# The first expert's low parts on VectorE around the row table, in a two-layer encoder on one Trainium2 core

## The reference

```
lg = x2 @ w_group + b_group            # the group of a token: argmax
le = x2 @ w_router + b_router          # its two experts within the group: top_k
...
order = jnp.argsort(flat_e)            # tokens sorted by expert, in blocks of rows
...
def expert_block(args):
    xb, e = args
    hid = jax.nn.silu(xb @ w_gate[e]) * (xb @ w_up[e])
    return hid @ w_down[e]
...
out = jnp.zeros_like(x2).at[slot_tok].add(ys * slot_w[:, None])
```

## Time and profile before

| | us |
|---|---|
| three runs | 2655.75, 2651.90, 2654.62 |
| median | 2654.62 |
| the profiled execution's own time | 2650.67 |
| its span, first to last instruction | 2649.0 |
| layer 0: first small DVE instruction behind the logits, first gate product | 502.60, 560.24 |
| the same in layer 1 | 1964.03, 2022.70 |
| busy by the page: PE, DVE, ACT, POOL | 2327.3, 1896.5, 1550.3, 331.2 |

### The profile page before, as it was taken

One profiled execution on the slowest core, in us unless ns is written; L12 is line 12 of the kernel. 1 busy time (PEld: TensorE's weight loads), 2 busy tenths in 40 slices (PEclk: granted clock), 3 DMA queues, 4 the chain that ended last, 5 costly groups with the idle time before them and its releaser, 6 DMA issues. The chain is left out here.

```text
span 2649.0 us, 34467 instructions
## 1 busy us (share of the span) xinstructions
PE 2327.3 (88%) x11464; PEld 1759.8 (66%) x11464; DVE 1896.5 (72%) x2453; ACT 1550.3 (59%) x2036; POOL 331.2 (13%) x268
## 2 busy tenths in 40 slices
PE   7899989459999999929999999998955999999991
PEld 5666658447777776727787777776843777777771
DVE  6775572668988888858566676556266988898885
ACT  5554450437787777725555555555042787778772
POOL 0000020211222111030000000002021222122102
PEclk9999999779999999969999999999976999999996
DMA  3013020649999999852000000002154999999995
GB/s 120 25 52 98 24 72 32 212 151 390 393 404 397 395 392 401 348 172 88 24 24 24 24 24 24 0 24 72 32 197 149 378 403 396 397 396 402 396 369 210
DMA packets 129503, 538.49 MB, mean 203 GB/s; under 512 B 23233, under 2 KB 52033, under 8 KB 80289
## 3 DMA queue, kind: packets, MB, share of 16 engines
q1 hardware_dynamic: 110496, 470.62, 46.7%
q0 software_dynamic: 18944, 67.12, 7.3%
HBM read 487.50 MB, written 50.20 MB: 203 GB/s over the span
## 5 line engine op out<-in xcount | busy, mean ns | idle before, releaser
L1508 DVE TENSOR_TENSOR m_lo_gate<-m_raw_gate,m_hi_gate 128x2048 fp32r<-128x2048 f32 x128 | 289.1, 2289 | 99.6 <-ACT m_hi_gate L1503 99.5
L1503 ACT CAST m_hi_down<-m_raw_down 128x2048 fp32r<-128x2048 f32 x124 | 236.2, 1906 | 106.6 <-PEq L848 67.1
L1508 DVE TENSOR_TENSOR m_lo_down<-m_raw_down,m_hi_down 128x2048 fp32r<-128x2048 f32 x124 | 279.5, 2283 | 10.6 <-ACT m_hi_down L1503 10.2
L1508 DVE TENSOR_TENSOR m_lo_up<-m_raw_up,m_hi_up 128x2048 fp32r<-128x2048 f32 x124 | 283.1, 2283 | 4.8 <-ACT m_hi_up L1503 4.3
L1503 ACT CAST m_hi_gate<-m_raw_gate 128x2048 fp32r<-128x2048 f32 x132 | 246.7, 1906 | 17.9 <-DMA m_raw_gate<-in_moe_w_gate_dram 17.9
L1503 ACT CAST m_hi_up<-m_raw_up 128x2048 fp32r<-128x2048 f32 x128 | 244.5, 1912 | 18.0 <-DMA m_raw_up<-in_moe_w_up_dram 17.1
L1622 PE MATMUL m_G<-m_hi_gate,m_x_hi 128*96 128x512 f32 x512 | 206.2, 403 | 11.4 <-DVE m_x_lo L1732 11.3
L1591 POOL DMA_INDIRECT m_xg<-hn_rows,m_pick x64 | 154.7, 2417 | 417.9 <-PE m_XT L1635 403.0
L1622 PE MATMUL m_U<-m_hi_up,m_x_hi 128*96 128x512 f32 x512 | 205.2, 401 | 0.0
L1623 PE MATMUL m_G<-m_hi_gate,m_x_lo 128*96 128x512 f32 x512 | 204.9, 400 | 0.0
L1624 PE MATMUL m_G<-m_lo_gate,m_x_hi 128*96 128x512 f32 x512 | 202.9, 396 | 0.0
(11 more groups left out here) (382 smaller groups left out, 4989.2 us busy)
## 6 DMA issues: line engine op xcount, KB each, us to landing
m_raw_gate<-in_moe_w_gate_dram SPq DMA_DIRECT2D x128, 1024.0 KB, 10.7
m_raw_up<-in_moe_w_up_dram SPq DMA_DIRECT2D x128, 1024.0 KB, 12.6
m_raw_down<-in_moe_w_down_dram SPq DMA_DIRECT2D x124, 1024.0 KB, 10.5
out_rows<-m_y POOLq DMA_DIRECT2D x64, 384.0 KB, 7.9
a1n_rows<-in_diff_w_qkv_dram SPq DMA_DIRECT2D x21, 512.0 KB, 5.3
out_rows<-a0n_gain SPq DMA_DIRECT2D x1, 8064.0 KB, 37.0
x_res<-in_x_dram SPq DMA_DIRECT2D x4, 1024.0 KB, 9.7
a0n_rows<-in_swa_w_o_dram SPq DMA_DIRECT2D x8, 512.0 KB, 3.3
```

Source lines behind the costliest of these rows:

```text
L1503: act.copy(self.hi[w][:, cut], self.raw[w][:, cut]).then_inc(self.hi_done[w], 1)
L1508: eng.tensor_tensor(self.lo[w][:, cut], self.raw[w][:, cut], self.hi[w][:, cut].bitcast(F32), ALU.subtract)\
```

## The change

DVE makes the four low parts of the first expert's gate and up that POOL made. The first (gate 0) stands in route, between the copy of `control` and the copy of the table. The second (gate 1) and third (up 0) stand at the start of run, ahead of `x_part(0)`. The fourth (up 1) stands behind `x_part(0)`, and so do the two of down, which stood ahead of it before. SP's four loads of expert 1's gate and up move from route into run, ahead of the two of down that stood there. POOL has no low part left.

```
@@ route, SP @@
                 for w in range(1, 3):
                     for piece in range(2):
                         moe.load(sp, w, piece, 0)
-                for w in range(2):
-                    for piece in range(2):
-                        sp.wait_ge(moe.lo_done[w], piece + 1)
-                        moe.load(sp, w, piece, 1)
                 norm.sync_stored(sp)
@@ route, POOL @@
-                for w in range(2):
-                    for piece in range(2):
-                        moe.low_part(pool, w, 0, piece)
@@ route, DVE @@
                 own(dve.tensor_copy(moe.control[:, :], ctl_f[0:1, :]))
+                moe.low_part(dve, 0, 0, 0)
                 dve.wait_ge(tabled, 1)
                 own(dve.tensor_copy(moe.table[:, :], L_ps[0:CAP, 0, 0:COLS]))
@@ run, SP @@
                     last = steady_blocks(sp) + 2
-                    for piece in range(2):
-                        load(2, piece, 1, 1)
+                    for w in range(3):
+                        for piece in range(2):
+                            load(w, piece, 1, 1)
@@ run, DVE @@
+                    self.low_part(dve, 0, 0, 1)
+                    self.low_part(dve, 1, 0, 0)
+                    x_part(0)
+                    self.low_part(dve, 1, 0, 1)
                     self.low_part(dve, 2, 0, 0)
                     self.low_part(dve, 2, 0, 1)
-                    x_part(0)
                     last = in_turn(dve, step)
```

## The result

| | before | changed |
|---|---|---|
| median of the runs, us | 2655.35 (6 runs) | 2639.65 (6 runs, 2634.28 to 2641.32) |
| ratio | | 0.9935, 95% interval 0.9924 to 0.9945 |
| the profiled execution's own time, span | 2650.67, 2649.0 | 2641.32, 2639.3 |

The changed kernel is faster by 0.65%, some 17 us (15 to 20 by the interval). The difference of the medians is 15.7.

The account below looks back on a forecast made before the run. In route, DVE's chain of small instructions was taken as the bound, its adds waiting for POOL; the experts' stage had PE busy and DMA saturated. -33.9 + 0.6 + 14.4 = -18.9 us gave 2635.7 against the median, range 2626 to 2643.

Parts of the forecast that it names:

- What is removed: Route: the eight adds of L987 no longer wait for POOL's low parts; 16.7 and 17.2 us, 33.9 in all.
- E: Start of run: the moment at which ACT starts behind the barrier, 550.91 and 2013.72 in the profile before.
- The low part in route: Route: DVE's low part of 2.3 us hides behind the table's matmuls in layer 1, overshoots by 0.6 in layer 0.
- The port at the start of run: Start of run: DVE's two low parts hold POOL's copy and first gather, issued by E + 6.1 instead of E + 3.0.
- The landing in company: Start of run: with three loads ahead, the first gather lands 7.1 us behind its issue instead of 3.17.
- What moves at no cost: Run, behind `x_part`: up 1, the two of down and the loads behind them cost nothing; the cover is 4 us.
- Held up less: Rival, 0.23 with its variants: loads at the start of run do not delay the first gather's landing; -26.7 us, 2627.9.
- The copy alone held: Rival, 0.09: at the start of run low parts delay POOL's copy but not the gather's issue; -22.1 us, 2632.5.
- The adds not held by POOL: Rival, 0.04: in route something else stretches the adds, 33.9 stays and 15.0 us are paid; 2669.6.
- The head start: Rival, 0.04: four loads leaving route's idle stretch are missed in the experts' stage, 21.2 us come back; 2656.9.
- More is paid than I see: Rival, 0.09: a second low part before POOL's copy, a later clock in block 0 or later landing; 5 to 12 us.

Follow-up runs that it names:

- the repetition: The changed kernel, unchanged, run again for a second profile: 0.9929 (0.9916 to 0.9943) against the kernel before, 18.8 us faster.
- the moved loads alone: The kernel before with only SP's four loads of expert 1's gate and up moved from route into run: 1.0041 (1.0026 to 1.0056), 10.9 us slower.
- the kernel before again: The kernel before, unchanged, run once more for a second profile: 2654.07 us.

## Why the prediction was right

Forecast 2635.7 with 2626 to 2643, measured 2639.65 in the six runs and 2634.94 in the five of the repetition. The working said -18.9 us, the ratios say -17.3 and -18.8, and the seams of the two profiles, where all of it was to happen, -18.2 and -18.6.

- **What is removed**, 33.9: 16.7 us in layer 0 as forecast. In layer 1 the way from the first instruction to E is 17.6 shorter, of which 17.3 are the adds. The rest is the clock: the table's matmuls took 4.73 us there and not the 5.44 of the kernel before, so that they ended ahead of the low part.
- **The low part in route**, 0.6 and 0: the way to E in layer 0 is 16.2 us shorter, which is 16.7 less 0.6. Right, with the reservation that the cover is the table's matmuls, and that their length depends on the clock, 4.3 to 5.4 us over the twelve profiles.
- **The port at the start of run**, E + 6.1 between 5.5 and 6.7: E + 5.5 in layer 0, E + 5.4 in layer 1. The first of the two orders happened in both layers: the copy came in between the two low parts. Only one of the two holds it, though they stand back to back. The prediction could not choose between the two orders and took the middle, 0.6 us too late. The Trainium skill (SBUF — State Buffer, Who interferes with whom) infers that such a `tensor_tensor` leaves descriptor generation alone. For the indirect DMA this does not settle the matter: its lengths of 2.20, 2.42, 2.41 and 3.07 us all follow from when a low part ends, and with no low part begun ahead of it it took 1.10. For GpSimd's direct DMA, the store of y, the trace agrees (0.52 to 0.56 us beside a low part, above). What the gather has and the store has not is the reading of its row numbers from `pick` in SBUF. That this is the part that waits fits both, and is not shown.
- **The landing in company**, 7.1: 8.38 and 8.18 us by the semaphores (8.44 in the row counts POOL's wait). This term was mis-sized. I took the middle of 5.94 and 8.08 because no load followed for a while. The missing load behind it bought nothing; the third gather, with three loads at the same distances, was the right row, with its 8.08. The high end of the landing and the low end of the port nearly cancelled, E + 13.9 and E + 13.5 against the E + 13.2 forecast, and that part of the agreement is luck. The first gate product moved by 7.8 us against E in each layer, 15.5 in all where 14.4 were forecast.
- **What moves at no cost**: up 1 and the two of down on DVE, the loads behind them. In the first profile block 0 took 17.8 and 18.3 us, before 18.7 and 18.0. Right.
- **The rivals.** Held up less: no, the gather landed 8.2 to 8.4 us behind its issue. The copy alone held: no, the gather was held as well. The adds not held by POOL: no, with one low part back on POOL one add is slow. The head start: the moved loads alone cost 10.9 us, 9.6 of it in the seam. More is paid than I see: in the first profile the rest of the program took 8.6 us longer, in the repetition it did not. Outside the two seams the twelve profiled executions took 2530 to 2541 us, whatever the kernel; the two of the changed kernel are the lowest and the highest of them, those of the kernel before 2533 and 2537. So that isn't the change. Why the blocks of one execution fall behind the loads at block 16 and those of another never do stays open.

## What to carry to other kernels

Work that reads SBUF, handed to GpSimd to relieve VectorE, relieved nothing here, because VectorE had `tensor_tensor` instructions with two SBUF inputs to run at the time: however small, each may wait for a whole instruction of GpSimd's, or for several (4.2 to 13.4 us for 0.19). The reverse holds too, so at a place where GpSimd must issue an indirect DMA that others wait for, VectorE's long instructions belong behind the start of that issue, tied to an instruction of GpSimd's engine and not to its queue. And the first gather of a stage goes out before the stage's bulk loads: here three such loads of 1 MB, none of them urgent, cost it 5 us in each layer.

## What the runs showed of the hardware

- A semaphore increment that stands behind an indirect DMA on GpSimd doesn't wait for its issue: VectorE ran 0.19 us ahead of the gather. With a memset behind the gather, which carries the increment, it started 0.16 us behind the gather's end, 541.91 against 541.75.
- The first gather, 384 KB, landed 2.9 to 3.2 us behind its issue on empty DMA engines, and 7.3 to 8.4 with three or four loads of 1 MB about it (by its semaphore). The DMA packets in the traces show two parts of this. On empty engines its first packet starts 0.7 us behind the issue and all of them take 1.7 to 2.0 us. With the loads the first packet starts 2.9 to 3.5 us behind the issue, and the packets take 3.2 to 4.7 us, side by side with those of the loads. It does not come after all that is queued: with the moved loads alone, about 1.5 MB of the four loads already issued had gone when its first packet went. Why the first packet waits stays open.
- A waiting GpSimd copy got in between two VectorE low parts that stand back to back, in both layers of the four profiles that have this order (1.55 and 1.72 us instead of 0.18). In the other direction that is not sure: of the adds beside POOL's four low parts only those of layer 0 in the first profile waited for one low part each. In layer 1 of it one add waited for three, 13.4 us, in the kernel before again one of each layer waited for two, 9.0 us, and with the moved loads alone there was one of either kind. The eight adds together took 18.5 to 19.1 us each time.
- An indirect DMA of GpSimd is held by a low part on VectorE that began ahead of it and ends 0.8 to 1.0 us behind that low part's end. One that begins behind its start, even by 0.01 us, does not hold it, and a direct DMA of the same size was not held at all.
